# Head norms and forgetting terms spread by one fp32r pass instead of an fp32 matmul

## The chip, the cores and the metric

The kernel runs on one core of a Trainium2 chip. The metric is the device time of one execution in microseconds (us). Three runs of the kernel before took 3422.69, 3422.86 and 3429.57 us, median 3422.86.

## The reference, cut to what matters

Two blocks of layers work on a sequence of T = 256 tokens with 1024 features: four layers of the first block (mixers hg, na, mla, hg) and two of the second (both with the mixer called branches). Every layer is a gated feed-forward network, a mixer and a second feed-forward network. The change touches only parts of the mixers: the root mean square norm of each head, and the forgetting attention of the second block.

```python
# every mixer: a norm of each head over its own 64, 96 or 128 features
y = xf * lax.rsqrt(jnp.mean(xf * xf, axis=-1, keepdims=True) + EPS)

# forgetting attention: a cumulative log gate is added to the logits
cum = jnp.cumsum(log_f, axis=1)
s = jnp.einsum("bqhd,bkhd->bhqk", q_blk, k) * (dh ** -0.5)
s = s + (c_blk[..., :, None] - cum_k[:, :, None, :])
s = jnp.where(kpos[None, :] <= qpos[:, None], s, NEG_INF_2)
p = jax.nn.softmax(s, axis=-1)
```

## The kernel before, in words

Activations lie with features on the 128 partitions and tokens along the row, so a chunk of 128 features holds two heads of 64. All large products are made of fp32r matmuls: weights and activations are each split in a high and a low part of type fp32r, and three matmuls (high by high, high by low, low by high) make one product. These are lines 443 to 445 in the mixers and 571 and 572 in the feed-forward networks. Small products (head statistics, attention scores, transposes) are plain fp32 matmuls.

The weights come as a stream of slabs of 128 x 2048 numbers. SyncE loads them in a ring of three, ScalarE makes the high part (line 1181), VectorE the low part (line 1656), TensorE uses it. The instruction order of every engine is written out by hand, with semaphores between them; nothing is scheduled by a program. A projection is called project(s): 48 matmuls into one of two PSUM banks, which VectorE has to have emptied before (`bank()` waits for `evac`).

A head norm goes in these steps:

1. ScalarE squares the projected chunks (line 1195, line 1268 for attention copies).
2. TensorE sums the squares of each head by a matrix of zeros and ones (`head_sums`, line 831; `output_sums`, line 749; `key_sums` and `query_sums`, lines 929 to 943). The sums of up to 8 heads land in 32 rows; a second set of 8 heads lands in the next 32 rows.
3. VectorE scales them (line 1679), ScalarE makes a guess of 1/sqrt by Ln and Exp (`root`, lines 1170 and 1172), VectorE does one Newton step (`inverse_root`, lines 1689 to 1691) and signals `root_ready`.
4. TensorE spreads each head's root over its 64 partitions: `spread` (line 841) and `spread_ropes` (line 891) multiply an fp32 matrix of zeros and ones of 8 rows by the 8 rows of roots, one matmul of 256 columns per chunk of 128 features.
5. VectorE multiplies the chunk by the spread roots in PSUM (`head_norms` line 1897, `normed_outputs` line 2004, `normed` lines 2163 and 2165).

Spreads stand at 4 places in hg (two in each of two layers, 4 matmuls each), 2 in na (8 each), 4 in mla (8, 4, 6 and 6) and 2 in the branches mixers (8 in each layer): 72 matmuls in all.

In the branches mixers the four rows of the cumulative gate, `br_cum`, and its negative, `br_ncum`, are added to the logits of heads 4 to 7 by two more fp32 matmuls of 4 rows per head and block of 128 queries (`br_scores`; issued in line 1048). The gate comes from one chunk of the projection (line 2266), a chain of VectorE and ScalarE instructions of 4 rows (lines 2276 to 2284).

`tables_of_start` (line 2484 onward) runs once on VectorE, at the end of the first feed-forward network; it turns constants from the buffer `start_const` into their final form.

Of the kernel before, what the change touches and what calls it, by code (L numbers as in the profile page):

```python
# [15 lines left out]
P = 128  # L16
T = 256
# [35 lines left out]
FOX_HEADS = 4  # L53
CONV_K = 31
# [67 lines left out]
def _consts():  # L122
    at = 0
    for name, width in (
        [("ident", P), ("ones", P), ("heads", 38), ("whole", 38), ("ropes", 36), ("spread", 4 * P), ("rot", P)]
        + [("cos", T), ("sin", T), ("namask", GRID_W), ("fxmask", TT * T), ("select", FOX_HEADS)]
    ):
        CONSTS[name] = (at, width)
        at += width
    return at  # L130
# [7 lines left out]
N_START = LEVELS + len(HALVES) * P  # L138
# [13 lines left out]
def build(nc, W, PRM, CST, START, RPB, XIN, OUT, TOE_ROWS, TOE):  # L152
    ctx = ExitStack()
    with ctx:
# [12 lines left out]
        cst = sb("cst", [P, N_CONSTS])  # L167
        x = sb("x", [P, KC, T])
# [23 lines left out]
        work = sb("work", [P, 10 * KC * T])  # L192

# [27 lines left out]
        toe_kept = sem("toe_kept")  # L221
        zeros_ready = sem("zeros_ready")
# [136 lines left out]
        br_x, br_l, br_cum, br_ncum = (region(3)[0:FOX_HEADS, 1024 + i * T:1024 + (i + 1) * T] for i in range(4))  # L359
# [8 lines left out]
        start_const = region(1)[:, 0:N_START]  # L368
# [63 lines left out]
        def _(pe):  # L432
# [240 lines left out]
            def hg(s):  # L673
# [69 lines left out]
                def output_sums(g):  # L743
                    b = stat_bank()
                    for j in range(2):
                        pe.wait_ge(sq_ready, c.up(sq_ready))
                        for i in range(2):
                            at = 2 * j + i
                            last = nc.tensor.matmul(b[0:32, 0, :], con("whole", 6 - 2 * at, 32), hg_sq[:, GROUP * g + at, :],
# [28 lines left out]

                own_tokens(0)
# [55 lines left out]
            def spread(q, chunks_out):  # L835

                for chunk, out in chunks_out:
                    g, at = chunk // 4, chunk % 4
                    a, _ = CONSTS["spread"]
                    rows = slice(32 * g, 32 * g + 8)  # L840
                    last = nc.tensor.matmul(out, cst[rows, a + at * P:a + (at + 1) * P], guess[rows, q, 0:T], start=True, stop=True)  # L841
# [44 lines left out]
            def spread_ropes(q, g, chunks_out):  # L886

                for at, out in chunks_out:
                    a, _ = CONSTS["spread"]
                    rows = slice(32 * g, 32 * g + 8)  # L890
                    last = nc.tensor.matmul(out, cst[rows, a + 2 * P * at:a + 2 * P * (at + 1):2], guess[rows, q, 0:T], start=True, stop=True)
                last.then_inc(spread_done, 1)

            def mla(s):
# [28 lines left out]
                def key_sums():  # L923
# [3 lines left out]
                    for g in range(2):  # L927
                        for at in range(4):
                            nc.tensor.matmul(b[32 * g:32 * g + 32, 0, :], con("heads", 6 - 2 * at, 32), ml_sqn[:, 4 * g + at, :],
# [1867 lines left out]
```

## Time and profile before

| | |
|---|---|
| median of 3 runs | 3422.86 us (3422.69 to 3429.57) |
| the profiled execution, its own time | 3428.15 us |
| its span | 3426.3 us |
| mean granted TensorE clock | 0.988 |
| TensorE (PE) busy | 3370.4 us, 98% |
| VectorE (DVE) busy | 2571.8 us, 75% |
| ScalarE (ACT) busy | 1651.7 us, 48% |
| GpSimd (POOL) busy | 187.3 us, 5% |
| chain that ended last | PE 93%, DVE 5%, ACT 1%, issue 1% |

Busy times of matmuls overlap and their ends are modelled, so what a matmul costs is read from the distance of starts, not from its mean duration. An fp32 matmul shows as two records, an fp32r matmul as one. The shape column of the profile gives the rows and columns of the weights that an instruction uses (8*128 is 8 rows and 128 columns), and a type f32 also where the operand is fp32r.

### The profile page before, as it was taken

The numbers are of one execution on the slowest core, as the hardware profiler recorded it, in microseconds if no ns is written. First come the engines' busy times: TensorE is split into PE (matmuls) and PEld (weight loads), VectorE is DVE, ScalarE is ACT, GpSimd is POOL, SyncE is SP. The second block draws the span as 40 slices with busy tenths as digits, with TensorE's granted clock in tenths as the row PEclk, the third lists the DMA queues.
The fourth block names the chain that finished last, engine by engine and source line by source line (L and its number), as shares of the span: only waits on it lengthen the run. The fifth ranks groups of instructions, "written<-read, shape, count | busy, mean of one in ns | idle before, by whom it ended". The sixth has DMA issues, their size and how long they took to land.

```text
span 3426.3 us, 59559 instructions
## 1 busy us (share of the span) xinstructions
PE 3370.4 (98%) x23844; PEld 3117.9 (91%) x23844; DVE 2571.8 (75%) x2982; ACT 1651.7 (48%) x1753; POOL 187.3 (5%) x158
## 2 busy tenths in 40 slices
PE   8999999999899999999999999999999999999999
PEld 8999999998799998699999989999999999999998
DVE  7778777775777777577877887777778777777876
ACT  4464445444545444444546444545445444454544
POOL 0100000110000000000000000000340000025000
PEclk9999999999999999899999999999999999999999
DMA  6553376554255554155554335455444545553454
GB/s 259 184 184 123 116 220 202 200 183 148 99 196 184 195 186 148 50 198 192 187 184 172 124 128 200 176 197 184 172 148 168 190 180 199 187 186 143 160 201 167
DMA packets 98937, 592.88 MB, mean 173 GB/s; under 512 B 25684, under 2 KB 26836, under 8 KB 27736
## 3 DMA queue, kind: packets, MB, share of 16 engines
q1 hardware_dynamic: 97280, 586.34, 47.8%
q10 hardware_dynamic: 1496, 4.20, 0.4%
q8 instruction: 125, 2.05, 0.2%
q14 instruction: 36, 0.29, 0.0%
HBM read 588.40 MB, written 2.11 MB: 172 GB/s over the span
## 4 chain that ended last, share of the span: by engine, by line
PE 93%; DVE 5%; ACT 1%; issue 1%; DMA 0%; DVEq 0%; SPq 0%; ACTq 0%
PE wide L571 25%; PE wide L572 13%; PE wide L443 9%; PE wide L444 8%; PE wide L445 8%; PE acc L445 7%; PE acc L444 7%; PE acc L443 7%; PE acc L716 1%; DVE low L1656 1%; PE acc L1048 1%; PE acc L646 1%; PE acc L841 1%; PE wide L657 0%; PE wide L831 0%
## 5 line engine op out<-in xcount | busy, mean ns | idle before, releaser
L1656 DVE TENSOR_TENSOR low<-raw,high 128x2048 fp32r<-128x2048 f32 x531 | 1215.5, 2292 | 229.5 <-ACT high L1181 227.4
L1181 ACT ACTIVATE high<-raw 128x2048 fp32r<-128x2048 f32 x550 | 1049.4, 1910 | 653.4 <-PE acc L445 363.7
L571 PE MATMUL wide<-xs,high 128*128 128x512 f32 x3840 | 1337.4, 390 | 0.0
L572 PE MATMUL wide<-xs,low 128*128 128x256 f32 x3840 | 1082.8, 282 | 0.0
L571 PEld LDWEIGHTS wide<-xs,high 128*128 128x128 f32 x3840 | 720.5, 188 | 148.3 <-issue 0.9
L572 PEld LDWEIGHTS wide<-xs,low 128*128 128x128 f32 x3840 | 725.8, 189 | 0.0
L444 PE MATMUL acc<-ends,high 128*128 128x256 f32 x2112 | 588.8, 279 | 0.0
L443 PE MATMUL acc<-ends,high 128*128 128x256 f32 x2112 | 588.8, 279 | 0.0
L445 PE MATMUL acc<-ends,low 128*128 128x256 f32 x2112 | 588.8, 279 | 0.0
L443 PE MATMUL wide<-xs,high 128*128 128x256 f32 x1912 | 549.8, 288 | 14.0 <-DVE low L1671 11.7
L444 PE MATMUL wide<-xs,high 128*128 128x256 f32 x1912 | 540.3, 283 | 0.0
L445 PE MATMUL wide<-xs,low 128*128 128x256 f32 x1912 | 539.7, 282 | 0.0
L443 PEld LDWEIGHTS acc<-ends,high 128*128 128x128 f32 x2112 | 397.1, 188 | 4.7
L445 PEld LDWEIGHTS acc<-ends,low 128*128 128x128 f32 x2112 | 397.1, 188 | 0.0
L444 PEld LDWEIGHTS acc<-ends,high 128*128 128x128 f32 x2112 | 397.1, 188 | 0.0
L443 PEld LDWEIGHTS wide<-xs,high 128*128 128x128 f32 x1912 | 366.6, 192 | 23.8 <-issue 22.6
L444 PEld LDWEIGHTS wide<-xs,high 128*128 128x128 f32 x1912 | 366.6, 192 | 0.6
L445 PEld LDWEIGHTS wide<-xs,low 128*128 128x128 f32 x1912 | 366.1, 191 | 0.0
L1240 ACT ACTIVATE gs<-wide 128x512 f32<-128x512 f32 x120 | 71.8, 598 | 421.9 <-PE wide L572 421.9
L1808 DVE TENSOR_TENSOR gs<-wide,gs 128x512 f32<-128x512 f32 x120 | 82.8, 690 | 211.7 <-ACT gs L1240 211.7
L443 PE MATMUL wide<-ends,high 128*128 128x256 f32 x600 | 175.9, 293 | 14.8 <-DVE gs L1733 4.0
L1242 ACT ACTIVATE sg<-gs 128x512 f32<-128x512 f32 x120 | 75.9, 632 | 201.9 <-DVE gs L1810 201.9
(232 smaller groups left out, 3548.5 us busy)
## 6 DMA issues: line engine op xcount, KB each, us to landing
raw<-stream SPq DMA_DIRECT2D x550, 1024.0 KB, 4.8
work<-rpb SPq DMA_DIRECT2D x16, 256.0 KB, 6.2
work<-bias_shifted ACTq DMA_DIRECT2D x2, 1024.0 KB, 4.8
cst<-consts SPq DMA_DIRECT2D x1, 1050.0 KB, 11.2
x<-x_in SPq DMA_DIRECT2D x1, 1024.0 KB, 4.9
raw<-stream SPq DMA_DIRECT2D x2, 512.0 KB, 7.0
work<-bias_by_distance ACTq DMA_DIRECT2D x2, 512.0 KB, 5.9
bias_shifted<-work ACTq DMA_DIRECT2D x1, 1024.0 KB, 3.9
```

The source lines that it names most:

```text
L443: nc.tensor.matmul(out, wh, ah, start=start, stop=False, **kw)
L444: nc.tensor.matmul(out, wh, al, start=False, stop=False, **kw)
L445: return nc.tensor.matmul(out, wl, ah, start=False, stop=stop, **kw)
L571: nc.tensor.matmul(out[:, n, :, :], wh, xs[:, :, k, :], start=(k == 0), stop=False, skip_group_check=True)
L572: last = nc.tensor.matmul(out[:, n, 0, :], wl, xh[:, k, :], start=False, stop=(k == KC - 1), skip_group_check=True)
L646: last = nc.tensor.matmul(acc[2 * (i % 2) + u][:, tt, :], lhs, rhs, start=(n == 0), stop=(n == terms - 1))
L716: last = nc.tensor.matmul(o, hg_km[:, h, tok], sides(hg_qy[:, h, tok], half), start=True, stop=True)
L1181: nc.scalar.activation(high[:, s % HIGH, :], raw[:, s % RAW, :], ACT.Copy).then_inc(high_ready, 1)
L1240: nc.scalar.activation(gs[:, :, :], gates[:, :, 1, :], ACT.Copy).then_inc(rest_copied, 1)
L1242: nc.scalar.activation(sg[:, :, :], gs[:, :, :], ACT.Sigmoid).then_inc(sig_ready, 1)
L1656: v.tensor_tensor(low[:, s % LOW, :], raw[:, s % RAW, :], high[:, s % HIGH, :].bitcast(F32), ALU.subtract).then_inc(low_ready, 1)
L1808: v.tensor_tensor(gs[:, :, :], gates[:, :, 0, :], gs[:, :, :], ALU.add).then_inc(vec_step, 1)
```

## The change

The roots are no longer used as fp32. VectorE writes each root twice: rounded to fp32r, and in full; then it subtracts the first from the second, so that a group of 64 rows holds the high parts in its first 32 rows and the low parts in its other 32. A matrix of zeros and ones that has its ones in both halves (`picks`, type fp32r, made once) spreads and adds both parts in a single fp32r matmul of 64 rows. To have each root in both halves, the matrices that sum the squares get 64 output columns instead of 32, and a second set of 8 heads lies at row 64. The gates of the forgetting attention are handled in the same way: the weight columns and the bias are repeated at rows 0, 32, 64 and 96, the whole chain runs on 100 rows, and each head uses 36 rows at row 0 or row 64, by whether its number is even or odd. The order of the work on every engine stays as it is; VectorE gets 25 instructions more, all other engines have the same list with other operands.

```diff
@@ tables (the constant block loses 260 columns, the start block gains 516) @@
+PICKS = LEVELS + len(HALVES) * P
+N_PICKS = 4 * P + FOX_HEADS
+N_START = PICKS + N_PICKS
+        picks = sb("picks", [P, N_PICKS], F32R)
+        roots = sb("roots", [P, 2, T], F32R)
-        start_const = region(1)[:, 0:N_START]
+        start_const = region(0, 2)[:, 0:N_START]
@@ TensorE: head_sums @@
-                    last = nc.tensor.matmul(b[32 * g:32 * g + 32, 0, :], con("heads", 6 - 2 * at, 32), squares_at[kind][j % 2][:, i, :],
+                    last = nc.tensor.matmul(b[64 * g:64 * g + 64, 0, :], con("heads", 6 - 2 * at, 64), squares_at[kind][j % 2][:, i, :],
@@ TensorE: spread (spread_ropes and the sums of hg and mla alike) @@
-                    rows = slice(32 * g, 32 * g + 8)
-                    last = nc.tensor.matmul(out, cst[rows, a + at * P:a + (at + 1) * P], guess[rows, q, 0:T], start=True, stop=True)
+                    rows = slice(64 * g, 64 * g + 64)
+                    last = nc.tensor.matmul(out, picks[rows, at * P:(at + 1) * P], roots[rows, q, :], start=True, stop=True)
@@ TensorE: br_scores @@
+                rows = slice(64 * (g % 2), 64 * (g % 2) + 32 + FOX_HEADS)
+                pick = picks[rows, 4 * P + g:4 * P + g + 1]
                 return [(br_q[half64(g), 2 + g // 2, tok], br_k[half64(g), 2 + g // 2, :]),
-                        (br_cum[0:FOX_HEADS, tok], con("select", g, 1, FOX_HEADS).to_broadcast([FOX_HEADS, T])),
-                        (con("select", g, 1, FOX_HEADS).to_broadcast([FOX_HEADS, P]), br_ncum[0:FOX_HEADS, :])]
+                        (roots[rows, 0, tok], pick.to_broadcast([32 + FOX_HEADS, T])),
+                        (pick.to_broadcast([32 + FOX_HEADS, P]), roots[rows, 1, :])]
@@ VectorE: in place of inverse_root at the 11 places that a spread follows @@
+            def head_roots(q, rows):
+                dve.wait_ge(guess_ready, c.up(guess_ready))
+                y, w, t = guess[0:rows, q, 0:T], var[0:rows, q, 0:T], newt[0:rows, 0:T]
+                link(v.scalar_tensor_tensor(t, y, -0.5, y, ALU.mult, ALU.mult))
+                link(v.tensor_tensor(t, t, w, ALU.mult))
+                v.scalar_tensor_tensor(roots[0:rows, q, :], t, 1.5, y, ALU.add, ALU.mult).then_inc(vec_step, 1)
+                v.scalar_tensor_tensor(y, t, 1.5, y, ALU.add, ALU.mult).then_inc(vec_step, 1)
+                dve.wait_ge(vec_step, c.up(vec_step, 2))
+                for g in range(rows // 64):
+                    part = slice(64 * g + 32, 64 * g + 64)
+                    last = v.tensor_tensor(roots[part, q, :], guess[part, q, 0:T], roots[part, q, :].bitcast(F32), ALU.subtract)
+                own(last, root_ready)
@@ VectorE: the gates of the forgetting attention @@
-                v.tensor_scalar(br_cum, br_l, 1.0, None, ALU.mult).then_inc(vec_step, 1)
-                c.up(vec_step)
-                own(v.tensor_scalar(br_ncum, br_l, -1.0, None, ALU.mult), norm_ready)
+                link(v.tensor_copy(br_cumr, br_l))
+                for at in (32, 96):
+                    part = slice(at, at + FOX_HEADS)
+                    last = v.tensor_tensor(br_cumr[part, :], br_l[part, :], br_cumr[part, :].bitcast(F32), ALU.subtract)
+                link(last)
+                own(v.tensor_scalar(br_ncumr, br_cumr.bitcast(F32), -1.0, None, ALU.mult), norm_ready)
@@ VectorE: tables_of_start @@
+                own(v.tensor_copy(picks[:, :], start_const[:, PICKS:N_START]), picks_ready)
```

`link` is an instruction followed by a wait for its own end; `own` is the same with another semaphore. `inverse_root` is linked three times. `head_roots` works on 64 rows in hg (4 times) and for the queries of mla (2 times), and on all 128 rows, with two subtractions, in na (2), for the keys of mla (1) and in the branches (2).

## Rows read from the trace of the kernel before

**Rows 1.** Groups by line and shape, TensorE: count, busy us, mean ns.
```profile
L841 PE MATMUL acc<-guess,cst 8*128 8x256 f32 x88 | 18.9, 415 | 0.5 <-DVE guess L1691 0.4
...
L1048 PE MATMUL acc<-cst,work 4*128 4x256 f32 x32 | 10.0, 434 | 0.0
L1048 PE MATMUL acc<-work,cst 4*128 4x256 f32 x32 | 9.1, 406 | 0.0
```

**Rows 2.** Timeline, all engines, na queries spread: start us, us, engine, line [idle before].
```profile
813.76 0.28 PE L444 MATMUL wide<-xs,high 128*128 128x256 f32 x1
...
814.58 0.27 PE L445 MATMUL wide<-xs,low 128*128 128x256 f32 x1
...
814.78 2.96 PE L841 MATMUL acc<-guess,cst 8*128 8x256 f32 x16
...
816.77 0.61 ACT L1195 ACTIVATE work<-work 128x512 f32<-128x512 f32 x1
...
817.68 1.42 PE L831 MATMUL wide<-work,cst 128*32 128x256 f32 x4
...
819.03 0.58 PE L443 MATMUL wide<-xs,high 128*128 128x256 f32 x1
```

**Rows 3.** Timeline of TensorE, scores of heads 4 and 5 in layer 5.
```profile
2474.66 0.70 PE L1048 MATMUL acc<-work 64*128 64x256 f32 x4
2475.29 1.13 PE L1048 MATMUL acc<-cst,work 4*128 4x256 f32 x4
...
2477.21 0.70 PE L1048 MATMUL acc<-work 64*128 64x256 f32 x4
```

**Rows 4.** Waits, longest first: engine, what for, us in total, times, longest us.
```profile
DVE acc L2297 <- PE acc L1048: 15.0, 4, 5.1
```

**Rows 5.** Timeline, branches in layer 5: the spread, and the values beside it.
```profile
2430.38 3.45 PE L841 MATMUL acc<-guess,cst 8*128 8x256 f32 x16
...
2430.56 1.27 DVE L1748 TENSOR_SCALAR work<-wide,rstdT 128x384 f32<-128x384 f32 x2 [3.07 <-PE wide L445]
```

**Rows 6.** Timeline, layer 6: the gate's chain and the work behind it.
```profile
3052.22 0.28 DVE L2282 TENSOR_SCALAR work<-work 4x256 f32<-4x256 f32 x1
...
3052.73 0.69 DVE L1733 TENSOR_TENSOR gs<-wide,rstd 128x512 f32<-128x512 f32 x1
...
3057.24 0.39 PE L443 MATMUL wide<-xs,high 128*128 128x256 f32 x1
```

**Rows 7.** Timeline, mla: the first queries' spread.
```profile
1372.76 0.68 DVE L2155 TENSOR_TENSOR gs<-wide,cst 128x512 f32<-128x512 f32 x1
...
1375.57 0.58 PE L443 MATMUL wide<-ends,high 128*128 128x256 f32 x1
```

**Rows 8.** Timeline, first hg layer: root, first spread, projection behind it.
```profile
347.80 0.41 DVE L1690 TENSOR_TENSOR newt<-newt,var 32x256 f32<-32x256 f32 x1
...
348.25 0.41 DVE L1691 SCALAR_TENSOR_TENSOR guess<-newt,guess 32x256 f32<-32x256 f32 x1
...
353.87 0.43 PE L443 MATMUL wide<-xs,high 128*128 128x256 f32 x1 [1.09 <-DVE work L2004]
```

**Rows 9.** Timeline, na keys: root, values, spread, next projection.
```profile
840.47 1.54 DVE L1748 TENSOR_SCALAR work<-wide,rstdT 128x512 f32<-128x512 f32 x2
...
840.58 2.93 PE L841 MATMUL acc<-guess,cst 8*128 8x256 f32 x16 [0.39 <-DVE guess L1691]
...
843.44 0.50 PE L443 MATMUL wide<-high,xs 128*128 128x512 f32 x1
```

**Rows 10.** Timeline of VectorE near the start: four instructions of 256 columns without waits.
```profile
11.25 1.67 DVE L1709 SCALAR_TENSOR_TENSOR xs<-x,prm,xs 128x256 fp32r<-128x256 f32 x4
```

**Rows 11.** Six stretches: length, PE, PEld, DVE, ACT, POOL busy, PE clock, DMA, GB/s.
```profile
2432.50:2439.60 7.10, 7.10 (x31) 6.37 (x31) 7.03 (x9) 0.00 (x0) 0.00 (x0) 0.52 0.59 213
...
sum 28.10, PE 28.10 PEld 25.58 DVE 24.96 ACT 9.33 POOL 16.22; mean PE 4.68 PEld 4.26 DVE 4.16 ACT 1.55 POOL 2.70
```

**Rows 12.** One longer stretch of the branches in layer 6, same columns.
```profile
3056.00:3082.00 26.00, 26.00 (x219) 24.88 (x217) 24.25 (x46) 14.53 (x27) 17.48 (x14) 1.00 0.46 163
```

More of the change, by code:

```diff
@@ L53 @@
 FOX_HEADS = 4
+FOX_ROWS = 96 + FOX_HEADS
 CONV_K = 31
@@ L124, in _consts @@
     for name, width in (
-        [("ident", P), ("ones", P), ("heads", 38), ("whole", 38), ("ropes", 36), ("spread", 4 * P), ("rot", P)]
-        + [("cos", T), ("sin", T), ("namask", GRID_W), ("fxmask", TT * T), ("select", FOX_HEADS)]
+        [("ident", P), ("ones", P), ("heads", 70), ("whole", 70), ("ropes", 68), ("rot", P)]
+        + [("cos", T), ("sin", T), ("namask", GRID_W), ("fxmask", TT * T), ("pad", 160)]
     ):
@@ L888, in spread_ropes @@
                 for at, out in chunks_out:
-                    a, _ = CONSTS["spread"]
-                    rows = slice(32 * g, 32 * g + 8)
-                    last = nc.tensor.matmul(out, cst[rows, a + 2 * P * at:a + 2 * P * (at + 1):2], guess[rows, q, 0:T], start=True, stop=True)
+                    rows = slice(64 * g, 64 * g + 64)
+                    last = nc.tensor.matmul(out, picks[rows, 2 * P * at:2 * P * (at + 1):2], roots[rows, q, :], start=True, stop=True)
                 last.then_inc(spread_done, 1)
@@ L928, in key_sums @@
                         for at in range(4):
-                            nc.tensor.matmul(b[32 * g:32 * g + 32, 0, :], con("heads", 6 - 2 * at, 32), ml_sqn[:, 4 * g + at, :],
+                            nc.tensor.matmul(b[64 * g:64 * g + 64, 0, :], con("heads", 6 - 2 * at, 64), ml_sqn[:, 4 * g + at, :],
                                              start=(at == 0), stop=False)
-                        last = nc.tensor.matmul(b[32 * g:32 * g + 32, 0, :], ones[0:ROPE, 0:32], ml_sqk[0:ROPE, :], start=False, stop=True)
+                        last = nc.tensor.matmul(b[64 * g:64 * g + 64, 0, :], ones[0:ROPE, 0:64], ml_sqk[0:ROPE, :], start=False, stop=True)
                     last.then_inc(stat_done, 1)
@@ L1404, in na @@
                 ahead(s + 8)
-                root(T, 64)
+                root(T, P)
                 n_stat[0] += 1
@@ L2616, in constants, with twice_wide @@
     t = np.arange(T)
+    def twice_wide(n):
+        cols = np.arange(n)[None]
+        return np.where(cols >= 32 + n - 64, cols - 32, cols)
     put("ident", np.eye(P))
     put("ones", np.ones((P, P)))
-    put("heads", (i[:, None] // 64 + 6 == np.arange(38)[None]) * 1.0)
-    put("whole", (np.arange(38)[None] // 2 == 3) * np.ones((P, 1)))
-    put("spread", (i[:, None] % 32 == np.arange(4 * P)[None] // 64) * 1.0)
-    put("ropes", (i[:, None] // ROPE + 4 == np.arange(36)[None]) * 1.0)
+    put("heads", (i[:, None] // 64 + 6 == twice_wide(70)) * 1.0)
+    put("whole", (twice_wide(70) // 2 == 3) * np.ones((P, 1)))
+    start[:, PICKS:PICKS + 4 * P] = i[:, None] % 32 == np.arange(4 * P)[None] // 64
+    put("ropes", (i[:, None] // ROPE + 4 == twice_wide(68)) * 1.0)
     half = ROPE // 2
@@ L2675, in by_chunk, with rows_twice @@
         return a.reshape(-1, P).T
+    def rows_twice(a):
+        wide = np.zeros((a.shape[0], P), np.float32)
+        for at in range(0, P, 32):
+            wide[:, at:at + FOX_HEADS] = a
+        return wide
     def twice(a):
```

73 lines of the change are left out of this document (37 added, 36 removed).

## The prediction

> **What bounds the kernel now.** I read the page first: TensorE is busy for 98% of the span and holds 93% of the chain that ended last. So a matmul taken away counts, unless TensorE then waits for another engine. Next come the groups by line, for how many records the change touches [rows 1]; then the timeline around each spread, for what TensorE does behind it [rows 2, 5, 7, 8, 9] and for the forgetting scores [rows 3, 6]; then the waits [rows 4] and the granted clock of stretches [rows 11]. The reader is to see two things. The fp32 matmuls that go are slow for what they do: 8 or 4 rows of 128. And at several of them TensorE would not have gone on sooner, since the next step hangs on VectorE or ScalarE.
>
> **Price of the matmuls.** Between 813.76 and 814.58 lie seven fp32r matmuls of 256 columns, 0.117 us each [rows 2]. The eight spreads of na show 16 records, and the next instruction starts 2.90 us after the first [rows 2]. Eight fp32r matmuls would take 8 x 0.117 = 0.94 us. No row shows an fp32r matmul of 64 weight rows. From below it is the 0.117 of full weights. From above it is the start distance of the fp32 records, 4 of them in the 0.97 us from 2475.29, with 0.3 us of changeover left out of it, so some 0.23 us [rows 3]. I take 0.12, because it has the type and the columns of the new one, and keep the other end.
>
> **Price on VectorE.** Linked instructions of 256 columns start 0.45 us apart [rows 8]; unlinked ones take (1.67 - 0.45)/3 = 0.40 us [rows 10]. A root of 64 rows gains one unlinked and one linked instruction, 0.85 us; one of 128 rows gains another unlinked subtraction, 1.25 us. The gate's chain had two unlinked instructions in the 0.51 us from 3052.22 to 3052.73 [rows 6]; now it is a linked copy (0.30), two subtractions (0.40 + 0.45) and a linked negation (0.30), 1.45 us: 0.9 us more.
>
> **Forgetting scores.** One block of queries for two heads repeats after 2477.21 - 2474.66 = 2.55 us: 0.63 us for q by k, 1.92 us for eight 4-row records [rows 3]. The q by k records of two heads lie at rows 0 and 64 and start almost together: four records in 0.70 us [rows 3]. The new 36-row matmuls lie in the same two halves, so I expect 2 x 0.12 us and 0.1 us more of changeover: 1.0 us per block, saved 1.5 us. If the halves don't overlap and each takes 0.23, the block saves 1.0. There are 2 blocks, 2 pairs of heads and 2 layers: 8 x 1.5 = 12.0 us (8.0 at the other end). VectorE waits for these scores, 15.0 us in four times [rows 4], so this is on the path.
>
> **Spreads of the branches.** Root and spread are 2.9 us apart, since the values' slabs lie between: VectorE has idled 3.07 us [rows 5], which hides the 1.25 us. The projection behind starts 1.95 us sooner, twice: -3.9 us. The gate's chain then ends 0.9 us later, and the second projection after it needs the bank that VectorE empties at 3052.73 to 3053.4, then 3054.3 [rows 6]. TensorE came there at 3057.24 [rows 6], so there are 2.9 us to give up before that wait appears. It limits what a better clock can bring here.
>
> **mla.** The keys' spread waits for its root, +1.25 against -1.95 us; the two sums that lie there leave -0.6. At the first queries' spread TensorE goes on at 1375.57 [rows 7]. With the spread short, it is VectorE that ends last: it empties the rotation's bank at 1372.76 + 0.68 = 1373.44 [rows 7], moved 0.25 us forward by the keys' gain less one root of 0.85. So 1373.2: -2.35 us in all up to there. The second queries' spread is in the attention, where VectorE is dense: -1.2 for the chain of three spreads, +0.85 for the root, -0.35. Sum -2.7 us.
>
> **hg.** Behind the first spread, project starts at 353.87 after 1.09 us of waiting for VectorE's line 2004 [rows 8]. VectorE works without a gap from the root to there. So the shorter spread is worth nothing, and 0.85 us is added: +1.7 us for two layers. Behind the second, root +0.85 and spread -0.9 lie in one chain: 0.
>
> **na.** Behind the first spread the sums wait for ScalarE's square, over at 816.77 + 0.61 = 817.38; TensorE was there at 817.68 [rows 2]. Gain 0.15 us in place of 1.96. Behind the second, VectorE's values (840.47, 1.54 us) come after the root and are 1.25 us later, 843.26, and TensorE needs them for the bank where it went on at 843.44 [rows 9]: 0.
>
> **Start.** The cast of 516 columns stands at the end of the first network, where VectorE is on the path to the next norm: 0.45 us by the 0.45 of a linked instruction, 0 to 1. The wider sums (64 columns for 32) keep count and moving columns: 0, at most 0.05 us for each of some 60.
>
> Sum without the clock: -12.0 - 3.9 - 2.7 + 1.7 - 0.15 + 0.45 = -16.6 us.
>
> **The clock.** Six stretches in the branches stand at 0.51 to 0.53 of the clock, the 1.2 GHz level, 28.1 us together [rows 11]. TensorE is busy in all of them, so they cost 13.5 us. Two begin about 2 us after a spread starts [rows 5, 11], the other four in or behind forgetting scores: matmuls of 8 or 4 rows precede each. These are what goes. I count 8 of the 13.5 us, because VectorE, busy for 24.25 of 26.00 us [rows 12], can't follow all of it. In na, mla and hg the spreads turn into waiting, and the low clock stays; I add 1.5 us for one new fall, since 3.5 us at half clock lose 1.7. Sum -6.5.
>
> The skill weighs against me here: the Trainium skill, TensorE: Matmul & The Clock Gate, section "HAM oscillation — how this bites in real kernels", has the clock fall through gaps between bursts of matmuls. By that rule only work counts, and spreads turned into waits can fall where there was no fall. In this trace the engine was not idle but on 8 rows when it fell; which of the two decides, the trace can't say.
>
> **Result.** The profiled execution took 3428.15 us; minus 23.1 is 3405.0. It lies 5.3 us above the median of the runs, to which the same difference gives 3422.9 - 23.1 = 3399.8, rounded 3400.
>
> **Rivals.**
> 1. *The clock stays as it is.* For it: a fall may hang on the waits and half-filled matmuls around, which stay. Against: nearby pairs of 64-row scores with transposes show no fall. 3422.9 - 16.6 = 3406.
> 2. *VectorE takes the place of TensorE.* For it: 93% busy in the branches' dense stretch [rows 12], and 0.9 us more in the gate's chain. Against: it waits for the scores [rows 4] and before the values [rows 5]. Then the branches' spreads and clock give nothing and half of the scores' gain goes: -6.0 - 2.7 + 1.7 + 0.3 = -6.7, 3416.
> 3. *64-row fp32r matmuls cost 0.23 us.* For it: a weight load may not hide behind a matmul of the same rows. -4.0 of the scores' gain, 16 x 0.11 = 1.8 in the branches, 0.6 in mla: 6.4 less gained, and the clock as forecast: 3406. The skill says it (TensorE: Matmul & The Clock Gate, "The mechanism": loads overlap matmuls in flight only in other row groups); the full-row fp32r matmuls at 0.117 us speak against.
> 4. *Slower: the clock falls in the new waits.* At each of 12 spreads and 4 pairs of forgetting scores TensorE now has fewer matmuls and the same waits. If every one of the 16 brings a further fall, at 1.7 us, that is +27.2 - 16.6 = +10.6: 3433. It decides from ten new falls on. Against: in the branches nothing waits behind the spread.
> 5. *The change doesn't do what it says* (the compiler keeps two records per matmul): the VectorE work alone, +1.7 + 1.25 + 0.85 + 2 + 0.45 = +6, 3429. Hardly likely.
>
> **Chances.** Forecast 0.50 (own range 3394 to 3405); rival 1 0.22; rival 2 0.13; rival 3 0.09; rival 4 0.04; rival 5 0.02. A difference under 0.2% (6.8 us) can't be told from none. Faster: forecast, 1, 3 and half of 2, 0.87. Same: the other half of 2 and most of 5, 0.08. Slower: 0.05. The range reaches down to all 13.5 us of clock and 2 more elsewhere, 3422.9 - 16.6 - 15.5 = 3391, taken as 3389, and up over rivals 1 and 3 to 3413.
>
> **What would show it.** Right: 72 spread matmuls and 32 of the gate in single records 0.12 us apart; a block of forgetting scores in 1.0 us; at least three of the six stretches back at 2.4 GHz; hg's projection behind the first spread 0.85 us later. Wrong: blocks of 1.5 us, new low stretches beside na's spreads, or TensorE waiting for VectorE behind the gate's chain in both layers for more than 3 us.

## The result, and the profile after

Four runs of the kernel after took 3396.28 to 3404.38 us, median 3400.24; four of the kernel before in the same set 3422.69 to 3429.57, median 3425.10. By the medians that is 24.9 us less; the ratio is 0.992, 95% interval 0.991 to 0.993, which is 23 to 32 us. Predicted were 3400 us, 22.9 less. The profiled execution took 3404.38 us against 3428.15 of before, 23.8 less, where the sum said 23.1. The sum is right as a whole; several of its terms are not, as the stages show.

From the page of the kernel after, the busy times and the chain that ended last:

```profile
PE 3326.7 (98%) x23740; PEld 3087.9 (91%) x23740; DVE 2592.1 (76%) x3014; ACT 1651.9 (49%) x1753; POOL 204.5 (6%) x158
...
PE 87%; DVE 9%; issue 2%; ACT 1%; DMA 0%; DVEq 0%; SPq 0%; ACTq 0%
```

104 records of TensorE are gone: 72 spreads and 32 gate matmuls take one record in place of two. VectorE has 3014 instructions in place of 2982, so 32 more and not the 25 that the section on the change gives: 11 copies, 16 subtractions, 4 for the gates and the cast. The groups by line and shape, answering to [rows 1]; the last column is idle time just before:

```profile
L848 PE MATMUL wide<-roots,picks 64*128 64x256 f32 x20 | 5.4, 354 | 4.3 <-DVE gs L1755 2.3 <-DVE roots L1713 1.2 <-DVE x L2039 0.4
L848 PE MATMUL acc<-roots,picks 64*128 64x256 f32 x44 | 4.4, 300 | 2.9 <-DVE roots L1713 2.9
...
L1054 PE MATMUL acc<-picks,roots 36*128 36x256 f32 x16 | 3.7, 458 | 0.0
L1054 PE MATMUL acc<-roots,picks 36*128 36x256 f32 x16 | 2.3, 280 | 0.0
```

Before, the spreads into acc stood 0.5 us idle; now 2.9, for VectorE's new last instruction (line 1713).

The timeline of TensorE and ScalarE in na, queries' spread, answering to [rows 2]:

```profile
818.33 0.75 PE L848 MATMUL acc<-roots,picks 64*128 64x256 f32 x8
819.01 1.08 PE L839 MATMUL wide<-work,cst 128*64 128x256 f32 x4
...
820.32 0.62 ACT L1203 ACTIVATE work<-work 128x512 f32<-128x512 f32 x1
```

Eight spreads take 0.68 us to the next start, where 2.90 stood. The sums at 819.01 do not wait for that square, which comes 1.3 us later.

The timeline of TensorE for heads 4 and 5 in layer 5, answering to [rows 3]:

```profile
2473.49 0.70 PE L1054 MATMUL acc<-work 64*128 64x256 f32 x4
2473.83 0.47 PE L1054 MATMUL acc<-picks,roots 36*128 36x256 f32 x2
2474.13 0.28 PE L1054 MATMUL acc<-roots,picks 36*128 36x256 f32 x2
2474.25 0.60 PE L1054 MATMUL acc<-work 64*128 64x256 f32 x4
```

A block of queries repeats after 0.76 us, not 2.55 and not the 1.0 forecast. VectorE's line 2322, which had waited 15.0 us in [rows 4], has no wait left in the trace.

The branches' spread [rows 5], and the gate's chain of layer 5 with the first forgetting scores beside it (layer 6 of [rows 6] looks alike):

```profile
2433.37 0.74 PE L848 MATMUL acc<-roots,picks 64*128 64x256 f32 x8
...
2434.32 0.36 PE L450 MATMUL wide<-xs,high 128*128 128x256 f32 x1 [0.20 <-DVE work L1770]
...
2445.33 0.29 DVE L2304 CAST roots<-work 100x256 fp32r<-100x256 f32 x1
2445.66 0.85 DVE L2307 TENSOR_TENSOR roots<-work,roots 4x256 fp32r<-4x256 f32 x2
2445.69 1.14 PE L1054 MATMUL acc<-work 64*128 64x256 f32 x8
2446.54 0.29 DVE L2309 TENSOR_SCALAR roots<-roots 100x256 fp32r<-100x256 f32 x1
2446.87 0.69 DVE L1755 TENSOR_TENSOR gs<-wide,rstd 128x512 f32<-128x512 f32 x1
...
2447.71 0.35 PE L450 MATMUL wide<-xs,high 128*128 128x256 f32 x1 [0.89 <-DVE gs L1755]
```

The projection follows the spread after 0.95 us; before, it was 2.9 us in layer 6 and 3.4 in layer 5, where the clock fell during the spread. The wait behind the gate's chain, priced at nothing, is there with 0.89 us in both layers.

hg's first spread, answering to [rows 8]:

```profile
352.33 0.50 PE L848 MATMUL wide<-roots,picks 64*128 64x256 f32 x2
...
353.99 0.50 PE L848 MATMUL wide<-roots,picks 64*128 64x256 f32 x2 [1.16 <-DVE gs L1755]
...
356.22 0.36 PE L450 MATMUL wide<-xs,high 128*128 128x256 f32 x1 [1.74 <-DVE work L2026]
```

Two waits, 2.9 us, where one of 1.09 stood. The second pair of spreads must wait for a bank, which VectorE empties in its own order, after the root.

### Where the time went: the six mixers

The windows of the six mixers, first of before, then of after. Columns: window, its length, busy time (count) of PE, PEld, DVE, ACT, POOL, granted clock, DMA, GB/s. The feed-forward networks between them differ by 0.2 us at most.

```profile
199.23:407.87 208.64, 201.19 (x1541) 191.42 (x1540) 166.56 (x222) 109.31 (x129) 5.91 (x4) 0.98 0.35 127
769.24:922.85 153.61, 141.96 (x996) 119.96 (x995) 96.12 (x197) 73.68 (x137) 0.00 (x0) 0.98 0.31 110
1284.45:1465.11 180.66, 169.15 (x1162) 136.89 (x1161) 118.55 (x197) 84.59 (x159) 0.00 (x0) 0.93 0.27 100
1826.69:2029.58 202.89, 197.77 (x1541) 188.40 (x1539) 165.69 (x221) 108.22 (x126) 5.96 (x4) 0.99 0.35 125
2391.03:2639.39 248.36, 245.26 (x1892) 231.97 (x1891) 190.26 (x263) 121.39 (x146) 67.23 (x61) 0.96 0.43 157
3000.98:3246.04 245.06, 242.19 (x1892) 230.01 (x1891) 191.19 (x263) 121.61 (x146) 68.61 (x61) 0.97 0.44 159
```

```profile
199.13:411.23 212.10, 201.45 (x1533) 192.56 (x1532) 168.73 (x227) 109.87 (x129) 5.88 (x4) 0.96 0.35 125
772.61:922.60 149.99, 136.31 (x980) 116.23 (x979) 98.58 (x203) 73.68 (x137) 0.00 (x0) 0.99 0.32 113
1284.17:1464.64 180.47, 161.99 (x1138) 132.29 (x1137) 121.27 (x204) 84.67 (x159) 0.00 (x0) 0.93 0.28 100
1826.23:2032.59 206.36, 198.14 (x1534) 189.66 (x1532) 167.31 (x225) 108.29 (x126) 5.71 (x4) 0.98 0.34 123
2393.97:2627.07 233.10, 227.51 (x1868) 218.46 (x1867) 196.22 (x268) 121.61 (x146) 76.70 (x61) 1.00 0.46 168
2988.66:3222.26 233.60, 228.76 (x1868) 219.90 (x1867) 196.31 (x268) 121.65 (x146) 76.75 (x61) 0.99 0.46 167
```

In order: hg, na, mla, hg, branches, branches. Their lengths differ by +3.5, -3.6, -0.2, +3.5, -15.3 and -11.5 us. The same subtraction for every kernel's profiled execution (what each kernel changes is told in the next section), and in brackets how much of the stage stood at 1.2 GHz (us, summed from the trace's clock record), is the table from which the experiments are read:

| kernel | hg | na | mla | hg | branches | branches |
|---|---|---|---|---|---|---|
| before | (10.2) | (6.8) | (23.9) | (3.4) | (20.5) | (13.7) |
| after | +3.5 (17.1) | -3.6 (3.4) | -0.2 (23.9) | +3.5 (10.2) | -15.3 (0) | -11.5 (3.4) |
| after_again | -0.2 (6.8) | -3.4 (3.4) | -1.2 (20.5) | +4.2 (13.7) | -15.2 (0) | -11.5 (3.4) |
| fox_only | -0.1 (10.2) | +1.8 (10.2) | +1.8 (27.3) | -0.1 (3.4) | -13.8 (3.4) | -8.1 (6.8) |
| roots_only | +2.4 (13.7) | -3.6 (3.4) | -0.1 (23.9) | +3.5 (10.2) | -3.2 (17.1) | -3.5 (10.2) |
| hg_old | 0.0 (10.2) | -2.1 (6.8) | +1.4 (27.3) | -0.1 (3.4) | -15.1 (0) | -11.3 (3.4) |
| f32_wide | +1.7 (10.2) | -0.8 (0) | -3.3 (10.2) | +3.1 (6.8) | -12.8 (0) | -9.2 (0) |
| narrow | +3.6 (17.1) | -2.0 (6.8) | +1.6 (30.7) | +3.5 (10.2) | -13.8 (3.4) | -10.9 (0) |
| high_only | -2.6 (3.4) | -4.6 (3.4) | -6.7 (13.7) | +0.7 (6.8) | -14.7 (3.4) | -11.5 (0) |
| high_half | -3.0 (3.4) | -4.9 (3.4) | -6.6 (13.7) | +0.9 (6.8) | -14.7 (3.4) | -11.6 (0) |
| hg_mla_full | +2.7 (13.7) | -3.6 (3.4) | -3.3 (10.2) | +3.1 (6.8) | -15.2 (0) | -11.5 (3.4) |
| halves | 0.0 (10.2) | -3.6 (3.4) | -3.0 (17.1) | -0.1 (3.4) | -15.1 (3.4) | -11.5 (3.4) |
| halves_na | -2.4 (3.4) | +0.3 (6.8) | -3.0 (17.1) | -1.4 (0) | -14.9 (3.4) | -11.6 (0) |
| pool_cast | -0.7 (6.8) | -3.5 (3.4) | -1.0 (20.5) | +0.6 (3.4) | -15.1 (0) | -11.5 (3.4) |

One trace each: the brackets of hg and mla move by 3 to 10 us between two runs of the same kernel (after, after_again), and the stage with them by up to 3.7. So a stage of hg or mla in one trace settles no difference of 1 or 2 us.

### The profile page after: what moved, and what is told of

Read it like the earlier page. It is cut to its first block, busy times and chain, and to the rows that moved or that the text cites. A ratio compares the mean times of both kernels' runs of the same rounds, so it can differ in the third digit from the quotient of the medians.

```text
span 3402.4 us, 59385 instructions
## 1 busy us (share of the span) xinstructions
PE 3326.7 (98%) x23740; PEld 3087.9 (91%) x23740; DVE 2592.1 (76%) x3014; ACT 1651.9 (49%) x1753; POOL 204.5 (6%) x158
## 4 chain that ended last, share of the span: by engine, by line
PE 87%; DVE 9%; issue 2%; ACT 1%; DMA 0%; DVEq 0%; SPq 0%; ACTq 0%
PE wide L578 26%; PE wide L579 14%; PE wide L450 7%; PE acc L452 7%; PE acc L451 7%; PE acc L450 7%; PE wide L452 7%; PE wide L451 7%; DVE low L1664 2%; PE acc L723 1%; DVE work L2350 1%; PE acc L653 1%; PE wide L664 1%; PE wide L839 0%; PE acc L728 0%
```

## The experiments

All were timed beside the kernel before, in three sets of kernels. Each ratio is to the runs of before of its own set. Medians of before: 3430.57 us in the first set (fox_only to f32_wide), 3426.41 in the second (after_again to hg_mla_full), 3426.56 in the third.

### The two parts apart

fox_only has after's forgetting terms and before's roots; roots_only the other way round.

```diff
 fox_only, spreads and roots
-                    rows = slice(64 * g, 64 * g + 64)
-                    last = nc.tensor.matmul(out, picks[rows, ...], roots[rows, q, :], ...)
+                    rows = slice(64 * g, 64 * g + 8)
+                    last = nc.tensor.matmul(out, picks[rows, ...].bitcast(F32), guess[rows, q, :], ...)
 roots_only, forgetting terms
-                        (roots[rows, 0, tok], pick.to_broadcast([32 + FOX_HEADS, T])),
+                        (br_cum[0:FOX_HEADS, tok], pick.to_broadcast([FOX_HEADS, T])),
```

> The forgetting terms as in the kernel after; the head roots and spreads as before (three linked VectorE instructions, fp32 matmuls of 8 rows), on sums of 64 columns. Theory A (parts add up, and each low-clock stretch belongs to the few-row matmuls ahead of it): 8 blocks of queries save 1.5 to 1.9 us each, 12 to 15 us; the four low stretches behind forgetting scores go (17.0 us, worth up to 8.5, of which I take 5), the two behind the branches' spreads near 2433 and 3044 stay; hg, na and mla stand as before, the cast adds 0.4. Together 17 to 20 us under the kernel before, 4 to 7 over the kernel after. Rival B (the clock follows the whole stage, so that the low stretches of the branches stay unless both parts are there): 12 to 15 us under before, with at least five of the six stretches kept.

> The head roots and spreads as in the kernel after; the forgetting terms as before (fp32 matmuls of 4 rows, VectorE's old chain). Theory A: branches' spreads -3.9 us and the clock of the two stretches behind them -3 to -5; na -3.6, mla -0.2, hg +5 to +7 as measured in the kernel after, cast 0.4: 1 to 5 us under the kernel before. A forgetting block stays at 2.55 us and the four low stretches behind them stay. Rival B: the branches keep all six stretches, and the time is that of the kernel before, +2 to -1 us. Fox-only and roots-only together should give the whole difference of -24 us within 3 us if the parts add.

Measured: fox_only 3409.41 us (3407.55 to 3412.31), ratio 0.994, interval 0.993 to 0.996; roots_only 3423.18 (3418.73 to 3428.95), 0.998, 0.997 to 0.999. That is -21.2 and -7.4 us to the median of before, each a little more than was expected, together -28.6, against -24.9 of after in its set and -21.7 in the second. The sum was to meet -24 within 3 us and misses that by 1.6; with runs of one kernel 5 to 12 us apart, this shows neither that the parts add exactly nor that they don't. In the branches fox_only gives 21.9 of the 26.8 us, roots_only 6.7. Granted clock behind the spread and behind the scores, windows of fox_only, then of roots_only:

```profile
2431.00:2440.00 9.00, 9.00 (x62) 8.17 (x61) 6.15 (x5) 3.47 (x2) 0.00 (x0) 1.00 0.29 102
3033.00:3037.00 4.00, 4.00 (x23) 4.00 (x22) 4.00 (x4) 0.00 (x0) 0.00 (x0) 0.57 0.47 190
```

```profile
2475.00:2483.00 8.00, 8.00 (x38) 7.10 (x37) 5.82 (x15) 3.29 (x11) 7.36 (x8) 0.57 0.42 152
2495.00:2503.00 8.00, 8.00 (x32) 6.23 (x31) 5.36 (x12) 2.04 (x6) 7.37 (x8) 0.57 0.29 118
```

With the old scores the low stretches behind them stay; with the old spread one of two stays, and the one of layer 5 is gone though its 8-row spread is there. Theory A holds for the scores and in half for the spreads; rival B (only both parts together bring the clock back) is out.

### Type and rows: f32_wide and narrow

```diff
 f32_wide
-        picks = sb("picks", [P, N_PICKS], F32R)
+        picks = sb("picks", [P, N_PICKS], F32)
-        roots = sb("roots", [P, 2, T], F32R)
+        roots = sb("roots", [P, 2, T], F32)
 narrow, spreads (scores alike: 36 rows to 4)
-                    rows = slice(64 * g, 64 * g + 64)
+                    rows = slice(64 * g, 64 * g + 8)
```

> The kernel after with the two tiles of roots and of the zeros-and-ones matrix as fp32 in place of fp32r: the same VectorE work, the same 64 and 36 rows, but two records for each matmul. Theory D (only the type sets the duration, only the rows of a matmul set the clock): the mechanical gain goes (+20 us), a forgetting block takes 1.9 to 2.6 us, but the branches' low stretches stay away: 3412 to 3420. Rival E (the clock falls with time spent in partly filled fp32 passes, whatever the rows): the stretches come back as well and VectorE's extra work is left over: 3427 to 3433. Rival F (rows set the duration, two passes of 64 rows in two halves of the array overlap): a block in 1.3 us or less, 3405 to 3410.

> The kernel after with fp32r matmuls that read 8 rows of roots in place of 64 and 4 rows of gates in place of 36. This leaves the low parts out of the spreads and the scores; VectorE still makes them. With the kernels before (fp32, few rows) and f32_wide (fp32, 64 rows: 29 us of low stretches, clock 0.996) it completes a square of type and rows. Theory G (few rows make the clock fall, even in a short pass): low stretches in the branches again, clock 0.990 or less, 3403 to 3408. Theory H (time spent on few rows makes it fall; 8 fp32r matmuls pass in under 1 us, too short to count): clock and time as the kernel after, within 2 us. Duration, all theories: a matmul of 8 rows takes what one of 64 rows takes.

Measured: f32_wide 3407.42 us (3406.37 to 3411.40), 0.994, 0.992 to 0.995; narrow 3404.63 (3402.28 to 3410.53), 0.993, 0.992 to 0.995, against 3404.73 for after_again beside it. TensorE in f32_wide, the same block of scores:

```profile
2472.81 0.70 PE L1054 MATMUL acc<-work 64*128 64x256 f32 x4
2473.34 0.60 PE L1054 MATMUL acc<-picks,roots 36*128 36x256 f32 x4
2473.78 0.60 PE L1054 MATMUL acc<-roots,picks 36*128 36x256 f32 x4
2474.21 0.60 PE L1054 MATMUL acc<-work 64*128 64x256 f32 x4
```

and its windows of the branches:

```profile
2392.02:2627.59 235.57, 231.75 (x1892) 222.05 (x1891) 195.01 (x268) 121.39 (x146) 74.14 (x61) 1.00 0.46 166
2989.18:3225.01 235.83, 232.00 (x1891) 222.32 (x1890) 194.94 (x268) 121.34 (x146) 74.14 (x61) 1.00 0.45 166
```

A block of scores takes 1.40 us though every matmul still has two records. So of the 1.79 us that a block gained, 0.64 come from the type and 1.15 from the rows: even heads at row 0 and odd ones at row 64, two running at a time, and 36 of them in place of 4. Place and number changed together. That the number counts too is seen in narrow, whose 4-row fp32r matmuls lie in the same two halves:

```profile
2477.61 0.70 PE L1054 MATMUL acc<-work 64*128 64x256 f32 x4
...
2478.66 0.70 PE L1054 MATMUL acc<-work 64*128 64x256 f32 x4
```

Its block takes 1.05 us where 36 rows take 0.76, against the expectation that 8 rows take what 64 take; for the spreads that held (0.68 us for eight in both). The 1.40 us are near rival F's price (1.3 or less), where theory D set 1.9 to 2.6, and the time, 3407.42, lies in F's range.

The clock is the best of all kernels, 0.996, and the branches have no low stretch. Their spreads show what the rows do: 16 fp32 records of 64 rows take the same 2.9 us as 16 of 8 rows, and nothing falls behind them. For the scores the comparison is less clean, since the block is also shorter (1.40 for 2.55 us). narrow shows another side: 8 rows in fp32r have after's time, and its branches stand low for 3.4 us in all (of before 34.2). So neither few rows alone nor fp32 alone makes the clock fall in the branches, but fp32 matmuls of few rows: 2.9 us of them at each spread, and 3.8 of the 5.1 us of two blocks of scores. Theory H says that it is their time; narrow changes the time and the type together, so that is in accord with the runs and not shown. D for the clock holds; E and G fall.

The Trainium skill (TensorE: Matmul & The Clock Gate, Part 3, "The mechanism") has matmuls in different row groups overlap. By that rule two gate matmuls, one in each half of the rows, take the time of one. The trace agrees: from the first gate record to the next q by k, 0.87 us in f32_wide (2473.34 to 2474.21) for 1.92 before.

### hg with its old spreads

```diff
-                        spread(q, [(2 * j + i, b[:, i, :]) for i in range(2)])
+                        spread(q, [(2 * j + i, b[:, i, :]) for i in range(2)], old=True)   # 8 rows, fp32, guess
-                    head_roots(q, 64)
+                    inverse_root(q, T, signal=root_ready, rows=64)
```

> The kernel after, with only hg's four root-and-spread places as before (16 fp32 matmuls of 8 rows, no extra VectorE work). Theory A (the predicted +0.85 us of VectorE for each of the two first spreads): 1.7 us under the kernel after, and hg's further loss of about 5 us, which comes with longer low-clock stretches, stays because it hangs on the start cast and on the waits around. Rival C (the low-clock stretches of hg hang on the short spreads, after which TensorE waits longer): 5 to 7 us under the kernel after, the stretches at 387 and 2009 back to half their length and the one at 1978 gone.

Measured: 3397.57 us (3394.79 to 3401.25, 4 runs), 0.990, 0.989 to 0.992. The median is 2.7 us under after's, in another set whose before ran 5.5 us slower, and the intervals of the two ratios overlap. In its trace both hg stages are back at the length of before, 7 us less than in the first trace of after, and 4 less than in after_again. Its timeline of the first spread, to be held against the one of after above:

```profile
349.80 2.00 PE L851 MATMUL wide<-guess,picks 8*128 8x256 f32 x8
...
352.90 0.36 PE L450 MATMUL wide<-xs,high 128*128 128x256 f32 x1 [1.11 <-DVE work L2029]
```

From the spread to the projection 3.1 us, in after 3.9: the predicted 0.8. The rest goes with the clock: in each of the two hg stages after has 6.8 us more at 1.2 GHz. na and mla of the same trace, whose code is that of after, moved by +1.5 and +1.6 with their clock, so the 7 us are one trace's. Of rival C's three signs two came, in the second hg layer (the stretch at 2009 halved, the one at 1978 gone); the one at 387 stayed at 6.8 us. The trace is nearer to rival C, the medians to theory A; the runs don't decide between them.

### VectorE's extra work: high_only, high_half

```diff
 head_roots in high_half (high_only with -0.5 and 1.5)
-                v.scalar_tensor_tensor(roots[0:rows, q, :], t, 1.5, y, ALU.add, ALU.mult).then_inc(vec_step, 1)
-                v.scalar_tensor_tensor(y, t, 1.5, y, ALU.add, ALU.mult).then_inc(vec_step, 1)
...
+                own(v.scalar_tensor_tensor(roots[0:rows, q, :], t, 0.75, y, ALU.add, ALU.mult), root_ready)
```

> The kernel after with head roots of three linked VectorE instructions that write only the fp32r part: the copy in full and the subtraction are left out, and so are the low parts of the roots (the rows that held them are written with the high parts, so that the spread roots are twice too large). This takes VectorE's extra 0.85 and 1.25 us away and leaves TensorE's work as in after. Theory A: hg's first spreads 0.85 us sooner each, na's second 1.25, mla's keys 1.25 and queries up to 0.85, branches 0: 3 to 5 us under the kernel after. Rival I (VectorE's extra work is hidden everywhere but in hg's first spreads): 1.7 us under.

> As high_only, with the constants of the root's two last steps halved, so that both groups of 32 rows hold half a root and the spread roots have their right size; rounded to fp32r, the low parts are left out. The TensorE and VectorE lists are those of high_only, only the values differ. Theory L (the 15 us that high_only gained come from VectorE's missing instructions, and from the clock that follows them): 3387 to 3392, mla 6 us and each hg stage 3 to 6 us shorter than in the kernel after. Rival M (the doubled roots made the gain, by saturated attention that switches fewer bits): 3398 to 3403.

Measured: high_only 3389.10 us (3388.24 to 3393.12, 4 runs), 0.989, 0.988 to 0.991; high_half 3385.29 (3384.18 to 3387.37, 4 runs), 0.988, 0.986 to 0.989. With roots of the right size it is no slower: rival M falls, and the time is under theory L's 3387 to 3392. high_only lies 15.6 us under after_again beside it, high_half 16.1 under pool_cast beside it. So the copies and subtractions, 11.3 us of VectorE in all by the prices of the prediction, cost some 15 us, three times the upper end of theory A; rival I falls too. The windows of hg (first) and mla in high_half:

```profile
198.52:404.12 205.60, 196.04 (x1532) 187.18 (x1532) 166.84 (x223) 109.70 (x129) 5.88 (x4) 0.99 0.36 129
...
1275.87:1449.95 174.08, 158.23 (x1136) 129.42 (x1136) 118.26 (x197) 84.53 (x159) 0.00 (x0) 0.96 0.29 103
```

mla is 6.4 us shorter than in after, with 10.2 us less at 1.2 GHz, and the hg stages 6.5 and 2.6; against after_again it is 5.4, 2.8 and 3.3.

### Full-row fp32 in hg and mla: hg_mla_full, halves, halves_na

hg_mla_full reads after's roots as fp32. halves makes them without the extra work: half a root in both groups of 32 rows, which the fp32 pass adds.

```diff
+                    if full:
+                        pick, root = pick.bitcast(F32), root.bitcast(F32)      # halves: guess[rows, q, :]
 halves (hg and mla; halves_na: na too)
+            def half_roots(q, rows):
+                dve.wait_ge(guess_ready, c.up(guess_ready))
+                link(v.scalar_tensor_tensor(t, y, -0.25, y, ALU.mult, ALU.mult))
+                link(v.tensor_tensor(t, t, w, ALU.mult))
+                own(v.scalar_tensor_tensor(y, t, 0.75, y, ALU.add, ALU.mult), root_ready)
```

> The kernel after with hg's and mla's spreads (40 matmuls) done as fp32 passes of 64 rows, two records each; na, branches and the forgetting scores stay fp32r. Theory J (in hg and mla the short spread turns into waiting, TensorE's activity drops, and the low stretches there get longer; full-row fp32 passes fill that time): low stretches in hg and mla fall from the 47.9 us in the trace of after to 20 to 25, as in f32_wide, worth 11 us; mla's spreads cost 2 to 3 us again; 3390 to 3396, 5 to 9 us under the kernel after. Rival K (the better clock of f32_wide came from na and the branches): no gain in hg and mla, 2 to 3 us over the kernel after.

> Head roots of hg and mla as three linked VectorE instructions in fp32 that give half a root in both groups of 32 rows, spread by fp32 matmuls of 64 rows (two records each), which add the halves; no copy and no subtraction. na, branches and forgetting scores as in the kernel after. It differs from hg_mla_full only by VectorE's missing 0.85 us (hg four times, mla's queries twice) and 1.25 us (mla's keys). Theory L (VectorE's extra work is on the path in hg and mla and brings low stretches with it): each hg stage 3 us under hg_mla_full, mla 1 to 2, together 7 us: 3390 to 3395. Rival N (only the hidden 1.7 us of hg's first spreads): 3398 to 3400.

> As halves, and na's spreads as fp32 halves of 64 rows as well. From the stage sums: na with fp32r spreads took 3.6 us less than before, with fp32 spreads of 64 rows 0.8 less, with high parts alone 4.6 less. Theory: na loses 2 of spread and gains 1.2 of VectorE: within 2 us of halves, more likely over than under. Rival O (what na gained was the low stretch behind its 8-row spread, and 64 fp32 rows bring that too): equal or 1 us under halves.

Measured: hg_mla_full 3400.28 us (3399.03 to 3403.14), 0.992, 0.991 to 0.994, 4.5 under after_again beside it; halves 3394.23 (3391.05 to 3399.02, 4 runs) and halves_na 3394.42 (3392.35 to 3397.29, 4 runs), both 0.990, 0.989 to 0.992. mla's attention in after, then in hg_mla_full:

```profile
1394.00:1412.00 18.00, 15.99 (x62) 9.07 (x62) 9.03 (x25) 7.40 (x27) 0.00 (x0) 0.53 0.00 0
```

```profile
1394.00:1412.00 18.00, 16.06 (x107) 9.44 (x104) 13.04 (x37) 10.16 (x36) 0.00 (x0) 1.00 0.01 1
```

In this trace the clock stands at full speed in the attention and mla ends 3.1 us sooner. The median is 4.5 us under after_again, just short of theory J's 5 to 9, and the stages stand low for 30.7 us in hg and mla, not 20 to 25 (in after it was 51.2, not the 47.9 of the expectation). In hg J failed: the stages stay 2.7 and 3.1 over before. halves, without VectorE's extra work, takes these away: 0.0 and -0.1, as theory L said; mla, where L set 1 to 2 us less, did not move (-3.0 for -3.3). And its attention ran low again, with the same slow spreads:

```profile
1395.00:1405.00 10.00, 10.00 (x40) 5.60 (x40) 5.06 (x17) 4.41 (x15) 0.00 (x0) 0.50 0.01 2
```

So mla stands at -3.0 to -3.3 in all four kernels with full-row fp32 spreads (f32_wide, hg_mla_full, halves, halves_na), 2 to 3 us under the traces of after, but that the slow spreads keep the clock up in the attention isn't shown. The table also shows where they lose: without VectorE's extra work on either side, mla stands at -6.6 with the fast fp32r spreads (high_half, whose low parts are left out) and at -3.0 with the slow ones (halves).

pool_cast, which is after with one instruction moved, ran beside halves and took 3401.37 us: halves is 7.1 us faster, and one run of its four (3399.02) lies above the lowest of pool_cast's five (3396.63). Against after itself, from other sets, it is 6.0 and 10.5 us, with ratio intervals that overlap in part. halves beats the kernel before for sure and the kernel after very likely. halves_na has the same time, but not the same stages: na is 3.9 us longer than in halves, more than the 2 us of its theory, so the reason that rival O gave falls, and the hg stages, whose code is the same, are 2.4 and 1.3 us shorter, with 6.8 and 3.4 us less at 1.2 GHz. That the whole came out even goes with the clock in hg, which the change doesn't touch.

### The cast on GpSimd

```diff
-                own(v.tensor_copy(picks[:, :], start_const[:, PICKS:N_START]), picks_ready)
+            nc.gpsimd.tensor_copy(picks[:, :], start_const[:, PICKS:N_START]).then_inc(picks_ready, 1)
```

> The kernel after with the cast of the zeros-and-ones matrix (516 columns) on GpSimd at its start, in place of VectorE at the end of the first network. Theory A: 0.45 us sooner into hg, in which case the low stretch near 207 may shorten by 3.4 us (1.7 us of time): 0.4 to 2 us under the kernel after, less than the runs' spread; the gap of TensorE near 205.7 falls from 1.79 to 1.4 us. Rival P (the cast hides in VectorE's idle time before the last network rows): the gap stays, no difference.

Measured: 3401.37 us (3396.63 to 3402.20), 0.992, 0.991 to 0.994: not to be told from after. But its place is clear. The first projection of hg, in after and in pool_cast:

```profile
205.68 0.36 PE L450 MATMUL wide<-xs,high 128*128 128x256 f32 x1 [1.51 <-DVE low L1679]
```

```profile
204.89 0.36 PE L450 MATMUL wide<-xs,high 128*128 128x256 f32 x1 [1.05 <-DVE low L1679]
```

Before waited 1.04 us there, after_again 1.54. The cast costs 0.46 us, as priced. The low stretch near 207 is gone in pool_cast, but in after_again too, which has the cast: that it hangs on the cast isn't shown.

### after_again

> The kernel after, unchanged, to stand beside the other kernels of this set on the same chip. Its earlier runs took 3396.3 to 3404.4 us at granted clocks of 0.994 to 0.991, so a step of 0.001 in the clock (3.4 us of the span) goes with some 2.7 us of time. All theories: 3396 to 3404.

Measured: 3404.73 us (3400.89 to 3405.70), 0.993, 0.992 to 0.995. Its median lies 4.5 us over that of the first set and 0.7 over the expected range, with before 1.3 over. Its trace is that of its fastest run (3400.89) and has 6.8 us less at 1.2 GHz in hg and 3.4 less in mla than the first trace of after: the clock there differs between runs of the same kernel.

## Why the prediction was right, point by point

- **64-row fp32r matmul, 0.12 us.** Right as a price, and rival 3 (0.23 us) is out. In mla's first queries' spread four such matmuls, all on one half of the rows, start 0.116 us apart (1371.91 to 1372.26). Not foreseen: where a spread uses both halves of the rows, two run at a time, and eight take 0.68 us instead of 0.94.
- **Forgetting scores, 1.0 us a block.** 0.76 us. The terms of a block were counted one behind the other, with 0.1 of changeover; the overlap of halves reaches over the changeover.
- **Branches' spreads, -1.95 each.** 0.95 us to the next projection where 2.9 stood: right.
- **The gate's chain, hidden.** Wrong in a small thing: TensorE waits 0.89 us for VectorE behind the first scores, in both layers. It had 2.9 us to give by [rows 6], but it now comes sooner by the spread's 1.95 us and by the clock, and VectorE's chain takes 1.0 us more.
- **Clock in the branches, 8 of 13.5 us.** Right in mechanism, too low in size. All six stretches are gone; the low time falls from 34.2 to 3.4 us, and the two stages give 26.8 us where 23.9 were forecast (12.0 + 3.9 + 8). Of that difference 2.3 us belong to the scores (8 x 1.79 = 14.3); with 3.9 for the spreads and 1.8 taken off for the two waits, some 10 us are left for the clock, an estimate. Rival 1 is out. The reason offered, few rows, had to be sharpened: few rows in fp32. It also holds for six of the eight low stretches only: the two at the ends of the stages (2603 and 3211, 6.8 us of the 34.2) begin behind waits of 2.0 us, and one of these is there in after. And of the two behind the spreads one began some 2 us after the spread's start, the other 3.3 us, when the spread was over.
- **na, -0.15.** Wrong, -3.6. The step that failed: that the sums behind the first spread wait for the square at 816.77. They use an earlier one; in after they start before that square. The spread was exposed, though the prediction's own rows allowed it only 0.3 us (817.68 less 817.38; it took 0.15): 2.2 us by the starts above (2.90 less 0.68), 3.5 with the low stretch near 818 that went with it. The second place gave 0.1, as forecast.
- **hg, +1.7.** Wrong in size: +7.0, and +4.0 in after_again. The 0.8 us at each first spread are there, and the start's 0.46 is in the first stage. The trade of root and spread at the second place came out as forecast: 3.65 us from TensorE's wait to the next projection (0.61 + 3.04, from 385.91), 3.77 before. What was left out is the clock, which moves by as much between two traces of the same kernel as the rest of the loss.
- **mla, -2.7.** -0.2 and -1.2 in two traces. The keys give -0.7 (forecast -0.6), taken between the starts of ScalarE's copies of the weight slabs. At the first queries the step that failed is VectorE's bank. It was to come 0.25 us sooner, "the keys' gain less one root"; but 0.6 less 0.85 is a loss, 1373.7 and not 1373.2, which would have made it -1.9 in place of -2.35. In after it is empty at 1374.36 where it was at 1373.44, and TensorE waits for it:

```profile
1373.68 0.68 DVE L2177 TENSOR_TENSOR gs<-wide,cst 128x512 f32<-128x512 f32 x1
...
1374.51 0.55 PE L450 MATMUL wide<-ends,high 128*128 128x256 f32 x1 [1.98 <-DVE gs L2177]
```

  Counted from the first slab of the stage (0.3 us sooner in after), the projection starts 0.8 us sooner. That one slab later it is -2.0 in all, near the forecast, is luck: the projection runs 1.2 us faster there, with 3.4 us at 1.2 GHz in place of 10.2. The attention behind gives 1.8 back, with 17.1 us at 1.2 GHz in place of 10.2.
- **Start, +0.45.** 0.46.
- **New falls, +1.5 for one.** Too low: each hg stage of the trace of after has 6.8 us more at 1.2 GHz than before, and mla's attention too; in after_again it is 3.4 less in the first hg stage and 10.3 more in the second. Rival 4 is right in kind (short spreads turned into waits cost clock), and far from the ten falls that it needed.

So -23.1 against -23.8 is right by luck, because the misses cancel: na and the branches 3.5 + 2.9 us better than forecast, hg and mla 5.3 + 2.5 us worse.

Before, the low stretches of hg began behind waits of 1.1 to 2.0 us, and three of the five in na and mla behind waits of 0.8 to 1.9; the ones at 818 (na) and 1350 (mla) began behind 8-row spreads with TensorE busy, as six in the branches did. Both kinds are in this kernel. The rule weighed in the prediction (the Trainium skill, TensorE: Matmul & The Clock Gate, "HAM oscillation — how this bites in real kernels": the clock falls through gaps between bursts) agrees with the first kind, and does not tell of the second, where TensorE was busy when it fell.

Open: how much of high_half's 15 us is VectorE's time and how much is the clock that follows, since no run holds one of them still; whether what makes the clock fall behind few rows is their time or the type; and why one 8-row spread of fox_only cost clock and the other didn't.

## What to carry to other kernels

A small matmul is worth its start distance times what TensorE really waits for behind it; look for the square, bank or root that the next instruction uses, and check that it is that very one. When a change takes TensorE time and gives VectorE time, put the VectorE part on the side where it is hidden: here the same device, with the gates, was worth 13 us a layer in the branches and cost 2 to 3.5 in hg. If the fast matmul needs operands that VectorE has to make first, count them in: a slower fp32 pass over roots that need no extra work (halves) was 7 us faster than the fast pass with it (pool_cast). And read a stage with low clock from more than one trace, since two traces of one kernel differed by as much as the effect.

## What the runs showed of the hardware

- fp32r matmuls of 64 rows in different halves of the array run two at a time even when issued one half after the other: eight in 0.68 us, and 0.116 us apart where all lie in one half.
- fp32 spreads of 8 and of 64 rows have the same price (16 records in 2.9 us) and a different effect on the clock: behind them the branches fell to 1.2 GHz in the kernel before and not in f32_wide (mean clock 0.988 and 0.996).
- Between 64-row matmuls, fp32r matmuls of 4 rows cost more than ones of 36 rows: a block of scores took 1.05 us in narrow, 0.76 in after.
- Run times of one kernel follow its mean granted clock: after took 3396.28 us at 0.994 and 3404.38 at 0.991.
